# Seven-product pairs in two of three down projections, other start addresses for their operands, and their additions moved to the end of the group

## The chip, the cores and the metric

The kernel runs on one core of a Trainium2 chip. It computes two transformer-like blocks on 256 tokens of width 2048, in float32 precision. The metric is the device time of one execution in microseconds (us). Before the change the median of three runs is 2616.38 us (2616.24 to 2616.57).

## The reference, cut to what matters

The change touches only the second block's feed-forward part, at the very end of the program. The hidden width is 5632 and the model width 2048:

```
hn = rms_norm_2(h, norm_ffn_g)
gate, up = jnp.split(hn @ w_gate_up, 2, axis=-1)
h = h + (jax.nn.silu(gate) * up) @ w_down
out = rms_norm_2(h, norm_final_g)
```

## The kernel before, in words

**Precision.** Every float32 operand is split into a high part (what the matmul's float32r format keeps) and a low part (the rest). A product is three matmuls: high by high, high by low, low by high. Weights arrive by DMA in `raw` (4 slots of two pieces each, 1 MB a slot), ScalarE copies a piece to `hi` (line 577), VectorE subtracts to get `lo` (line 941). `hi` and `lo` are rings of 4 pieces. The splits run 3 pieces ahead of TensorE (`AHEAD`), and a piece's `hi` and `lo` may be written only when TensorE has used the piece four before it.

**A piece** is 256 rows of a weight matrix by 512 columns. A group is one block of 512 output columns over all rows of a stage. Groups alternate between PSUM banks 0 to 3 and 4 to 7.

**The end of the program** is six stages: `f2_up0`, `f2_down0`, `f2_up1`, `f2_down1`, `f2_up2`, `f2_down2`. An up stage computes four (the last: three) blocks of 512 hidden columns, and the down stage behind it multiplies these by their rows of `w_down` into four groups of 512 output columns. A group of `f2_down0` and `f2_down1` has 8 pieces, one of `f2_down2` has 6. In a down stage the tokens (in `B`, high and low part) are the stationary operand and the weights stream past, 512 columns at a time. An ordinary piece is 2 (blocks of 128 rows) by 2 (halves of the tokens) by 3 matmuls, lines 1616 to 1618. Three such matmuls, one of each line, are called a triple below; an ordinary pair of pieces is 8 triples.

**The seven-product pair.** Pieces 2 and 3 of every down group except the very last one are worked as a pair, by a Strassen-like scheme in `seven_products`: 2x2 blocks of tokens times 2x2 blocks of weights need 7 products in place of 8. That is 14 products of 3 matmuls, 42 matmuls of 256 columns (lines 1757 to 1759) in place of 24 of 512. Eleven pairs are worked so: 4 in `f2_down0`, 4 in `f2_down1`, 3 in `f2_down2`. They need:

- sums of the activations, `s_form`, once for each down stage. VectorE and ScalarE make them in `activation_sums`, behind the second `up` group of the up stage.
- sums of the weight blocks, `t_sum`, made in `block_sums` by four VectorE operations (lines 957 to 961) behind the split of piece 1, and split into `t_hi` (ScalarE, line 584) and `t_lo` (VectorE, line 945) behind the split of piece 3. The second of the four operations changes a raw block, so ScalarE's split of piece 2 waits for it.
- five VectorE additions (lines 969 to 974) and one ScalarE copy (line 589) in `combine`, which bring two extra PSUM banks into the result `HT`. They stand at piece 5 of the group (`j == SEVEN_AT + 3`). The result's other two banks are added at the group's end (`evacuate`, kind `tpart` or `tlast`, line 1174).

At the end of a `tlast` group (`f2_down2`) VectorE also waits for ScalarE's squares of the result (line 650) and multiplies by the final gain (line 1186), before it goes on splitting. The very last group is worked in two token halves (`last_pieces`, lines 1805 to 1807).

**Order.** Each engine's program is written out by `walk`: for piece p it first splits up to piece p+3, then does what belongs to p. So at the last piece of a group an engine splits piece 2 of the next group, then evacuates the group, then splits piece 3 of the next and the block sums.

**Addresses.** SBUF tensors lie one behind the other in the order of their declarations, each start rounded up to 32 bytes. From the declared sizes: `hi` and `lo` have the same start modulo 256; call it 0. Then `A` and the rows of `B` start at -64 (`B` is 67,776 bytes behind `hi`, 264 x 256 + 192, and a row of `B` is 9 x 256 bytes). The tokens start `TOKEN_AT` = 16 floats into a row, so at 0. `s_form` is at -64, and `t_hi` and `t_lo` are at +64 (167,232 bytes behind `hi`, 653 x 256 + 64).

Of the kernel before, what the change touches and what calls it, by code (L numbers as in the profile page):

```python
# [45 lines left out]
TOKEN_AT = 16  # L46
# [203 lines left out]
def bass_two_blocks(nc, ins, out):  # L250
    SEGS, TOTAL = schedule()
    PAIRS = seven_product_pairs(SEGS)

    with ExitStack() as ctx:
# [26 lines left out]
        s_form, t_sum = overlay(s_form=([P, 2, 4, 2, P], F32R), t_sum=[P, 2, 3, SEVEN_COLS])  # L281
# [8 lines left out]
        small = sb("small", [P, 64])  # L290
        r_fin = sb("r_fin", [P, T])
# [18 lines left out]
        _, t_hi, t_lo = overlay(gfin_end=[P, MT * T + 3 * D], t_hi=([P, 2, 3, SEVEN_COLS], F32R), t_lo=([P, 2, 3, SEVEN_COLS], F32R))  # L310
# [185 lines left out]
        def walk(eng, tallies, split, evacuate, side, each_turn, combine, activation_sums, last):  # L496

            at = {"split": AHEAD}  # L500

            for seg in SEGS:
                def run(turn, t):
                    base = seg.p0 + (t or 0) * seg.per_turn

                    def split_to(end):

                        while at["split"] < end:
                            n = turn * seg.per_turn + seg.p0 + at["split"]
                            if not isinstance(n, int) or n < TOTAL:  # L510
                                split(n, base + at["split"])
                            at["split"] += 1

                    for g, kind in enumerate(seg.kinds):
                        G = turn * len(seg.kinds) + seg.g0 + g
                        for j in range(seg.pieces):
                            p = g * seg.pieces + j
                            split_to(p + 1 + AHEAD)
                            b0 = 4 * ((seg.g0 + g + (t or 0) * len(seg.kinds)) % 2)
                            if t is not None and j == SEVEN_AT + 3 and base + g * seg.pieces + SEVEN_AT in PAIRS:  # L520
                                combine(PAIRS[base + g * seg.pieces + SEVEN_AT], b0, turn * len(seg.kinds) + g)
                            if j == seg.pieces - 1:
# [8 lines left out]
                                evacuate(kind, G, end, b0, turn * len(seg.kinds) + g, first_tile(seg, turn, g), more,  # L531
                                         token_parts if seg.name.startswith("f2") else B_parts)
                                if sums:
                                    activation_sums(more)
                                assert left[0] == 0, (kind, left)
                            if (seg.name, p) in EACH_TURN:
                                each_turn(EACH_TURN[seg.name, p], turn)
                            if t is not None and t == 0:
                                for step in SIDE.get((seg.name, p), ()):
                                    side(step, G, lambda: split_to(at["split"] + 1))  # L540
                    at["split"] -= seg.per_turn


                lead = 0
                if seg.turns > 1:
                    steady = AHEAD + MORE.get(seg.kinds[-1], 0)
                    lead = 0 if at["split"] == steady else 1
                turns_of(eng, seg, tallies, run, lead)
            last()


        @block.scalar
        def _(act):
# [12 lines left out]
            def split(n, slot):  # L566

                raw_slot = slot // 2 % RAWS
                if isinstance(n, int):
                    act.wait_ge(raw_landed[raw_slot], landed(n // 2))  # L570
                elif slot % 2 == 0 or slot < AHEAD:
                    act.wait_ge(raw_landed[raw_slot], turn_landed(n, slot))
                if not isinstance(n, int) or n >= RING:
                    act.wait_ge(pieces_used, n - RING + 1)
                if isinstance(n, int) and n in PAIRS:
                    act.wait_ge(t1_set, PAIRS[n] + 1)
                act.activation(hi[:, slot % RING], raw[:, raw_slot, 2 * (slot % 2):2 * (slot % 2) + 2, :],  # L577
                               ACT.Copy).then_inc(hi_ready, 1)
                if isinstance(n, int) and n - 1 in PAIRS:
                    q = PAIRS[n - 1]  # L580
# [10 lines left out]
            def activation_sums(more):  # L591
# [3 lines left out]
                given.mark(act.activation(s_form[:, 0], pb_copy[:, :, :].rearrange("p f (i c) -> p f i c", i=2), ACT.Copy))  # L595
# [25 lines left out]
            def evacuate(kind, G, end, b0, gi, k, more, to_b):  # L621
# [294 lines left out]
            walk(act, {1: asked, 2: given, 3: ready}, split, evacuate, side, lambda quarter, turn: None, combine, activation_sums, last)  # L916
# [3 lines left out]
        def _(dve):  # L920
# [15 lines left out]
            def split(n, slot):  # L936
# [6 lines left out]
                if isinstance(n, int) and n - 1 in PAIRS:  # L943
                    dve.wait_ge(t_hi_ready, PAIRS[n - 1] + 1)
# [4 lines left out]
            def block_sums(n):  # L949

                w = raw[:, n // 2 % RAWS, :, :].rearrange("p (i e) (s c) -> p i e s c", e=2, s=2)
                dve.wait_ge(raw_landed[n // 2 % RAWS], landed(n // 2))
                dve.wait_ge(h_turned, 16)
                if PAIRS[n]:
                    dve.wait_ge(t_lo_ready, PAIRS[n])
# [6 lines left out]
                dve.wait_ge(t1_set, PAIRS[n] + 1)  # L962

            def combine(q, b0, gi):
# [6 lines left out]
                dve.tensor_tensor(x[:, 0, :], x[:, 0, :], work[:, 0:2, :].rearrange("p s c -> p (s c)"), ALU.add)  # L971
# [4 lines left out]
            def activation_sums(more):  # L976
# [10 lines left out]
                dve.tensor_tensor(s_form[:, 1], pb_copy[:, :, :].rearrange("p f (i c) -> p f i c", i=2), s_form[:, 0],  # L987
# [32 lines left out]
            def evacuate(kind, G, end, b0, gi, k, more, to_b):  # L1020
# [149 lines left out]
                elif kind in ("tpart", "tlast"):  # L1170
# [3 lines left out]
                    dve.tensor_tensor(x, x, ps[:, b0:b0 + 2, :], ALU.add).then_inc(psum_free, 1)  # L1174
# [343 lines left out]
            walk(dve, {0: own, 1: asked, 2: given, 3: ready}, split, evacuate, side, turn_h, combine, activation_sums, last)  # L1518
# [3 lines left out]
        def _(pe):  # L1522
# [71 lines left out]
            def piece(seg, g, j, slot, b0, n, steps=None):  # L1594
# [7 lines left out]
                for kk in range(2):  # L1602
                    k = 2 * j + kk + (4 * WIDEST_FIRST[g] if seg.name == "pool" else 0)
                    first = j == 0 and kk == 0
                    final = (j == seg.pieces - 1 or isinstance(n, int) and n == TOTAL - RING - 1) and kk == 1
# [145 lines left out]
            def seven_products(j, slot, b0, n):  # L1751

                Xh, Xl = token_parts
                half = SEVEN_COLS

# [8 lines left out]
                def summed(f, i):  # L1764
                    return s_form[:, 0, f, i, :], s_form[:, 1, f, i, :]
# [9 lines left out]
                pe.wait_ge(s_ready, PAIRS[n] // 4 + 1)  # L1775
                for i in range(2):
                    k = 2 * (j + i)
                    pe.wait_ge(lo_ready, n + i + 1)
                    product(p16[:, 0:half], i == 0, False, tokens(0, k), *block(0, 0, i))
                    product(z0[:, 0:half], False, False, tokens(0, k + 1), *block(1, 0, i))  # L1780
                    product(z0[:, half:GC], False, False, summed(3, i), *block(1, 1, i))
                    product(p57[:, 0:half], i == 0, False, summed(0, i), *block(0, 1, i)).then_inc(pieces_used, 1)
                pe.wait_ge(t_lo_ready, PAIRS[n] + 1)
                for i in range(2):
                    k = 2 * (j + i)
                    product(p16[:, half:GC], False, i == 1, summed(1, i), *block_sum(1, i))
                    product(p57[:, half:GC], False, i == 1, summed(2, i), *block_sum(0, i))
                    last = product(z1[:, 0:half], False, False, tokens(1, k + 1), *block_sum(2, i))
# [24 lines left out]
            for seg in SEGS:  # L1813
                def run(turn, t):
                    for g, kind in enumerate(seg.kinds):
# [10 lines left out]
                        for j in range(seg.pieces - RING if at_end else seg.pieces):  # L1826
# [9 lines left out]
                            if isinstance(n, int) and n in PAIRS:  # L1836
                                seven_products(j, slot, b0, n)
# [47 lines left out]
```

## Time and profile before

| | us |
|---|---|
| median of 3 runs | 2616.38 |
| profiled execution | 2616.46 |
| its span | 2614.7 |
| `f2_down0`, TensorE | 2061.4 to 2146.5 |
| `f2_down1`, TensorE | 2321.1 to 2406.2 |
| `f2_down2`, TensorE | 2537.2 to 2607.6 |
| tail behind the last matmul | 2607.6 to 2614.7 |

The profiled execution takes 1.8 us more than its span (what lies before the first and behind the last recorded instruction). "Busy" is the time in which an engine had an instruction under way. A matmul is recorded with its latency, longer than its share of the stream; the rate is read from the starts of successive matmuls.

### The profile page before, as it was taken

To read this page: it belongs to the slowest core of one execution; us is meant where nothing else is said; L and a number is where in the kernel's file an instruction comes from. 1 tells how busy PE (TensorE), PEld (TensorE's weight loads), DVE (VectorE), ACT (ScalarE), POOL (GpSimd) and SP (SyncE) were. 2 spreads that over 40 slices of the span, in tenths; PEclk is the share of its full clock that TensorE was granted. 3 is DMA by queue.
4 is the path that set the end of the run, shared out by engine and by line. 5 is a ranking of instruction groups with operands and counts; after the bars stand their busy time and mean duration, and the time that the engine had idled before them with its cause. 6 is when DMAs were issued, how large, how long until landed. Compare 5 with 4: busy or idle time off the path is not lost.

```text
span 2614.7 us, 50642 instructions
## 1 busy us (share of the span) xinstructions
PE 2602.3 (100%) x21534; PEld 2551.2 (98%) x21534; DVE 1694.6 (65%) x1817; ACT 1187.4 (45%) x1284; POOL 14.6 (1%) x33
## 2 busy tenths in 40 slices
PE   9999999999999999999999999999999999999998
PEld 8989999999999999999999999999999989998997
DVE  7668765555555556795676666556777875677567
ACT  5356554434443444465443433444544444444444
POOL 2000000000000000000000000000000000000000
PEclk9999999999999999999999999999999999999999
DMA  9654566565655565555555555555565555556553
GB/s 306 202 168 163 196 193 196 187 201 187 200 186 200 188 199 193 179 203 195 180 184 189 193 182 190 193 193 194 193 210 194 193 198 193 191 195 205 194 179 129
DMA packets 254461, 504.31 MB, mean 193 GB/s; under 512 B 9390, under 2 KB 11456, under 8 KB 254160
## 3 DMA queue, kind: packets, MB, share of 16 engines
q1 hardware_dynamic: 250160, 496.27, 56.8%
q10 hardware_dynamic: 3136, 4.21, 0.5%
q8 instruction: 131, 2.15, 0.3%
q0 software_dynamic: 992, 1.34, 0.2%
q14 instruction: 42, 0.34, 0.0%
HBM read 498.89 MB, written 2.89 MB: 192 GB/s over the span
## 4 chain that ended last, share of the span: by engine, by line
PE 99%; DVE 1%; issue 0%; ACT 0%; POOL 0%; DVEq 0%; ACTq 0%; POOLq 0%
PE ps L1579 49%; PE ps L1590 25%; PE ps L1637 4%; PE ps L1646 4%; PE ps L1641 3%; PE ps L1616 3%; PE ps L1618 3%; PE ps L1617 3%; PE ps L1757 1%; PE ps L1759 1%; PE ps L1758 1%; PE ps L1626 1%; PE ps L1627 1%; PE ps L1624 1%; DVE lo L941 0%
## 5 line engine op out<-in xcount | busy, mean ns | idle before, releaser
L941 DVE TENSOR_TENSOR lo<-raw,hi 128x1024 fp32r<-128x1024 f32 x939 | 1139.7, 1224 | 792.6 <-ACT hi L577 779.2
L577 ACT ACTIVATE hi<-raw 128x1024 fp32r<-128x1024 f32 x939 | 988.4, 1059 | 1208.0 <-PE ps L1590 924.3
L1579 PE MATMUL ps<-A,hi 128*128 128x256 f32 x7286 | 902.8, 276 | 0.0
L1579 PEld LDWEIGHTS ps<-A,hi 128*128 128x128 f32 x7286 | 861.1, 188 | 0.3
L1579 PE MATMUL ps<-B,hi 128*128 128x256 f32 x3963 | 491.0, 276 | 0.0
L1590 PE MATMUL ps<-A,lo 128*128 128x256 f32 x3648 | 487.7, 276 | 0.0
L1579 PEld LDWEIGHTS ps<-B,hi 128*128 128x128 f32 x3963 | 468.3, 188 | 0.1
L1590 PEld LDWEIGHTS ps<-A,lo 128*128 128x128 f32 x3648 | 447.5, 188 | 0.0
L1590 PE MATMUL ps<-B,lo 128*128 128x256 f32 x1984 | 265.2, 276 | 0.0
L1590 PEld LDWEIGHTS ps<-B,lo 128*128 128x128 f32 x1984 | 243.3, 188 | 0.0
L1637 PE MATMUL ps<-B,hi 128*128 128x260 f32 (+3 forms) x768 | 109.1, 284 | 0.0
L1646 PE MATMUL ps<-B,lo 128*128 128x258 f32 (+3 forms) x768 | 108.7, 284 | 0.0
L1641 PE MATMUL ps<-B,hi 128*128 128x256 f32 x768 | 104.1, 278 | 0.0
L1637 PEld LDWEIGHTS ps<-B,hi 128*128 128x128 f32 x768 | 100.0, 189 | 0.0
L1646 PEld LDWEIGHTS ps<-B,lo 128*128 128x128 f32 x768 | 98.9, 189 | 0.0
L1616 PE MATMUL ps<-hi,B 128*128 128x512 f32 x248 | 96.8, 390 | 0.0
L1618 PE MATMUL ps<-hi,B 128*128 128x512 f32 x248 | 96.6, 389 | 0.0
L1617 PE MATMUL ps<-lo,B 128*128 128x512 f32 x248 | 96.5, 389 | 0.0
L1641 PEld LDWEIGHTS ps<-B,hi 128*128 128x128 f32 x768 | 96.3, 188 | 0.0
L676 ACT ACTIVATE B<-work 128x1024 f32 (+1 forms) x26 | 27.6, 1063 | 72.5 <-DVE work L1081 64.6
L1618 PEld LDWEIGHTS ps<-hi,B 128*128 128x128 f32 x248 | 46.5, 188 | 10.0
L1617 PEld LDWEIGHTS ps<-lo,B 128*128 128x128 f32 x248 | 46.6, 188 | 9.2
(306 smaller groups left out, 1589.5 us busy)
## 6 DMA issues: line engine op xcount, KB each, us to landing
raw<-in_w_in_dram SPq DMA_DIRECT2D x135, 1024.0 KB, 5.1
raw<-in_ffn_w_dram SPq DMA_DIRECT2D x132, 1024.0 KB, 5.1
raw<-in_w_gate_up_dram SPq DMA_DIRECT2D x88, 1024.0 KB, 5.0
raw<-in_w_down_dram SPq DMA_DIRECT2D x44, 1024.0 KB, 5.0
raw<-in_w_out_dram SPq DMA_DIRECT2D x16, 1024.0 KB, 5.1
raw<-in_pl_w_gate_dram SPq DMA_DIRECT2D x16, 1024.0 KB, 5.1
raw<-in_conv_out_w_dram SPq DMA_DIRECT2D x16, 1024.0 KB, 5.0
raw<-in_w_o_dram SPq DMA_DIRECT2D x16, 1024.0 KB, 5.0
```

The source lines that it names most:

```text
L577: act.activation(hi[:, slot % RING], raw[:, raw_slot, 2 * (slot % 2):2 * (slot % 2) + 2, :], ACT.Copy).then_inc(hi_ready, 1)
L676: given.mark(act.activation(some((A_parts if kind == "cb" else to_b)[0], k, 4, 0, T), work[:, :, :], ACT.Copy))
L941: dve.tensor_tensor(lo[:, slot % RING], raw[:, slot // 2 % RAWS, 2 * (slot % 2):2 * (slot % 2) + 2, :], hi[:, slot % RING], ALU.subtract). ...
L1579: pe.matmul(ps[:, b0 + m, 0:T], high(slot, kk, m), x, start=j == 0 and kk == 0 and part == 0, stop=False)
L1590: last = pe.matmul(ps[:, b0 + m, 0:T], low(slot, kk, m), Xh, start=False, stop=j == seg.pieces - 1 and kk == 1)
L1616: pe.matmul(to, Xh, hi[:, slot % RING, kk, :], start=first, stop=False)
L1617: pe.matmul(to, Xh, lo[:, slot % RING, kk, :], start=False, stop=False)
L1618: last = pe.matmul(to, Xl, hi[:, slot % RING, kk, :], start=False, stop=final)
L1624: pe.matmul(to, Wh, Xh, start=first and m % 2 == 0, stop=False, skip_group_check=True)
L1637: pe.matmul(ps[:, b0 + m, 0:with_lo], high(slot, kk, m), B[:, 2 * j + kk, 0:with_lo], start=first and kk == 0, stop=False, skip_group_chec ...
L1641: pe.matmul(ps[:, b0 + m, 0:T], high(slot, kk, m), B_low[:, 2 * j + kk, :], start=False, stop=False, skip_group_check=True)
L1646: last = pe.matmul(ps[:, b0 + m, 0:with_hi], low(slot, kk, m), B[:, 2 * j + kk, 0:with_hi], start=False, stop=final and kk == 1, skip_grou ...
```

## The change

Four things are changed.

1. The pairs are now listed by stage, `PAIRS_AT`, for `f2_down0` and `f2_down1` alone. The three pairs of `f2_down2` become ordinary pieces, and the activation sums behind `f2_up2` go.
2. Addresses: `TOKEN_AT` becomes 0, so the tokens start at -64 in the count above. `t_hi` and `t_lo` start 48 floats (192 bytes) later, at 0. `s_form` has room for a second set (not used) and keeps its start; `t_sum` moves to the place of `r_fin`, `sumsq` and the tensors behind them, and `block_sums` no longer waits until `h` has been transposed.
3. `combine` moves from piece 5 to the group's end. VectorE first adds the two ordinary banks (as line 1174 did), then makes the five additions; the last of them frees the banks.
4. The start and stop flags and the indices are written for a list of pairs (`u` counts them in a group); with one pair in a group they come out as before.

```diff
-TOKEN_AT = 16
+TOKEN_AT = 0
...
-SEVEN_AT = 2
+PAIRS_AT = {"f2_down0": (2,), "f2_down1": (2,)}
+SUMS_BEHIND = {"f2_up0": (1,), "f2_up1": (1,)}
...
+def down_groups(segs):
+    return [(x, x.p0 + turn * x.per_turn + g * x.pieces)
+            for x in segs if x.name in PAIRS_AT for turn in range(2) for g in range(2)]
...
-    first = [x.p0 + turn * x.per_turn + g * x.pieces + SEVEN_AT
-             for x in segs if x.name.startswith("f2_down") for turn in range(2) for g in range(2)]
-    return {n: q for q, n in enumerate(first[:-1])}
+    pairs, groups = {}, {}
+    for i, (x, first) in enumerate(down_groups(segs)):
+        for u, j in enumerate(PAIRS_AT[x.name]):
+            pairs[first + j] = (len(pairs), sum(len(PAIRS_AT[f"f2_down{c}"]) for c in range(int(x.name[-1]))) + u, u)
+        groups[first] = (i, len(pairs) - 1)
+    return pairs, groups
...
-        s_form, t_sum = overlay(s_form=([P, 2, 4, 2, P], F32R), t_sum=[P, 2, 3, SEVEN_COLS])
+        s_form, = overlay(s_form=([P, 2, 2, 4, 2, P], F32R))
...
+        t_sum, = overlay(t_sum=[P, 2, 3, SEVEN_COLS])
         r_fin = sb("r_fin", [P, T])
...
-        _, t_hi, t_lo = overlay(gfin_end=[P, MT * T + 3 * D], t_hi=...
+        _, t_hi, t_lo = overlay(gfin_end=[P, MT * T + 3 * D + 48], t_hi=...
...
-                            if t is not None and j == SEVEN_AT + 3 and base + g * seg.pieces + SEVEN_AT in PAIRS:
-                                combine(PAIRS[base + g * seg.pieces + SEVEN_AT], b0, turn * len(seg.kinds) + g)
                             if j == seg.pieces - 1:
-                                sums = seg.name.startswith("f2_up") and kind == "up" and t == SEVEN_AT // 2
+                                behind = SUMS_BEHIND.get(seg.name, ())
+                                sums = kind == "up" and t in behind
+                                seven = SEVEN_GROUPS.get(base + g * seg.pieces) if t is not None else None
...
             def block_sums(n):
...
-                dve.wait_ge(h_turned, 16)
...
-            def combine(q, b0, gi):
-                x = HT[:, :, gi * GC:(gi + 1) * GC]
+            def combine(c, q, b0, x):
                 p1, v5, v7, u2 = (work[:, i, :] for i in range(4))
-                dve.wait_ge(p1_copied, q + 1)
+                dve.wait_ge(t_used, q + 1)
+                own.mark(dve.tensor_tensor(x, x, ps[:, b0:b0 + 2, :], ALU.add))
+                dve.wait_ge(p1_copied, c + 1)
                 step(dve.tensor_tensor(u2, p1, ps[:, b0 + 2, SEVEN_COLS:GC], ALU.add))
...
-                step(dve.tensor_tensor(x[:, 1, SEVEN_COLS:GC], x[:, 1, SEVEN_COLS:GC], ps[:, b0 + 3, 0:SEVEN_COLS], ALU.add))
+                return dve.tensor_tensor(x[:, 1, SEVEN_COLS:GC], x[:, 1, SEVEN_COLS:GC], ps[:, b0 + 3, 0:SEVEN_COLS], ALU.add)
...
-                    dve.tensor_tensor(x, x, ps[:, b0:b0 + 2, :], ALU.add).then_inc(psum_free, 1)
+                    if seven:
+                        combine(*seven, b0, x).then_inc(psum_free, 1)
+                    else:
+                        dve.tensor_tensor(x, x, ps[:, b0:b0 + 2, :], ALU.add).then_inc(psum_free, 1)
```

## Rows read from the trace of the kernel before

**Rows 1.** The page, parts 1 (busy time of each engine) and 4 (last chain).

```profile
PE 2602.3 (100%) x21534; PEld 2551.2 (98%) x21534; DVE 1694.6 (65%) x1817; ACT 1187.4 (45%) x1284; POOL 14.6 (1%) x33
...
PE 99%; DVE 1%; issue 0%; ACT 0%; POOL 0%; DVEq 0%; ACTq 0%; POOLq 0%
```

**Rows 2.** Windows, `f2_down2`: us, PE, PEld, DVE, ACT, POOL busy, PEclk, DMA share, GB/s.

```profile
2537.00:2607.70 70.70, 66.96 (x345) 56.93 (x344) 58.68 (x69) 34.04 (x48) 0.00 (x0) 0.98 0.34 122
```

**Rows 3.** Timeline, TensorE, pairs 2 and 3 of `f2_down2`: start, duration, instruction, idle before.

```profile
2558.47 0.28 PE L1757 MATMUL ps<-hi,B 128*128 128x256 f32 x1
...
2562.01 0.39 PE L1757 MATMUL ps<-hi,B 128*128 128x256 f32 x1 [1.99 <-DVE lo L941]
...
2567.31 0.40 PE L1616 MATMUL ps<-hi,B 128*128 128x512 f32 x1
...
2578.23 0.28 PE L1757 MATMUL ps<-hi,B 128*128 128x256 f32 x1
...
2580.60 0.39 PE L1757 MATMUL ps<-hi,B 128*128 128x256 f32 x1 [0.82 <-DVE lo L941]
...
2584.56 0.40 PE L1616 MATMUL ps<-hi,B 128*128 128x512 f32 x1
```

**Rows 4.** Windows: a part of pair 2 of `f2_down2`.

```profile
2563.36:2566.77 3.41, 3.41 (x17) 3.25 (x17) 3.41 (x4) 2.32 (x3) 0.00 (x0) 0.50 0.82 295
```

**Rows 5.** Timeline, TensorE, the last group of `f2_down2`.

```profile
2596.61 0.39 PE L1807 MATMUL ps<-hi,B 128*128 128x512 f32 x1
2597.80 0.50 PE L1805 MATMUL ps<-hi,B 128*128 128x512 f32 x1 [0.80 <-DVE lo L941]
```

**Rows 6.** Timeline, VectorE, end of the first group of `f2_down2`.

```profile
2556.97 1.22 DVE L1174 TENSOR_TENSOR HT<-HT,ps 128x1024 f32<-128x1024 f32 x1
2559.60 1.23 DVE L1186 TENSOR_TENSOR HT<-HT,gfin_row 128x1024 f32<-128x1024 f32 x1 [1.40 <-ACT pb_copy L650]
```

**Rows 7.** Timeline, TensorE, the pair of the second group of `f2_down0`.

```profile
2088.13 0.28 PE L1757 MATMUL ps<-hi,B 128*128 128x256 f32 x1
...
2088.84 0.28 PE L1757 MATMUL ps<-hi,s_form 128*128 128x256 f32 x1
...
2089.52 0.28 PE L1757 MATMUL ps<-hi,B 128*128 128x256 f32 x1
...
2090.92 0.28 PE L1757 MATMUL ps<-t_hi,s_form 128*128 128x256 f32 x1
...
2093.05 0.40 PE L1616 MATMUL ps<-hi,B 128*128 128x512 f32 x1
```

**Rows 8.** Timeline, TensorE, `f2_down0`: two starts with 36 matmuls between them.

```profile
2117.77 0.39 PE L1616 MATMUL ps<-hi,B 128*128 128x512 f32 x1
...
2125.93 0.39 PE L1616 MATMUL ps<-hi,B 128*128 128x512 f32 x1
```

**Rows 9.** Timeline, TensorE, stage `g`: two starts with 42 matmuls between them.

```profile
151.15 0.39 PE L1616 MATMUL ps<-hi,A 128*128 128x512 f32 x1
...
160.77 0.39 PE L1616 MATMUL ps<-hi,A 128*128 128x512 f32 x1
```

**Rows 10.** Timeline, ScalarE, first group of `f2_down0`: high part of the next group's piece 1.

```profile
2077.51 1.06 ACT L577 ACTIVATE hi<-raw 128x1024 fp32r<-128x1024 f32 x1 [1.39 <-PE ps L1618]
```

**Rows 11.** Timeline, VectorE, from piece 5 of the first group of `f2_down0`.

```profile
2077.02 0.41 DVE L969 TENSOR_TENSOR work<-work,ps 128x256 f32<-128x256 f32 x1
...
2079.98 1.23 DVE L941 TENSOR_TENSOR lo<-raw,hi 128x1024 fp32r<-128x1024 f32 x1
...
2083.80 1.23 DVE L941 TENSOR_TENSOR lo<-raw,hi 128x1024 fp32r<-128x1024 f32 x1
2084.94 1.21 DVE L1174 TENSOR_TENSOR HT<-HT,ps 128x1024 f32<-128x1024 f32 x1
2086.07 1.22 DVE L941 TENSOR_TENSOR lo<-raw,hi 128x1024 fp32r<-128x1024 f32 x1
2087.21 1.75 DVE L945 TENSOR_TENSOR t_lo<-t_sum,t_hi 128x1536 fp32r<-128x1536 f32 x1
```

More of the change, by code:

```diff
@@ L494, in first_tile, with walk @@
             return (turn * len(seg.kinds) + g) * MT
-        def walk(eng, tallies, split, evacuate, side, each_turn, combine, activation_sums, last):
+        def walk(eng, tallies, split, evacuate, side, each_turn, activation_sums, last):
             at = {"split": AHEAD}
@@ L531, in run @@
                                 evacuate(kind, G, end, b0, turn * len(seg.kinds) + g, first_tile(seg, turn, g), more,
-                                         token_parts if seg.name.startswith("f2") else B_parts)
+                                         token_parts if seg.name.startswith("f2") else B_parts, seven)
                                 if sums:
-                                    activation_sums(more)
+                                    activation_sums(more, behind.index(t))
                                 assert left[0] == 0, (kind, left)
@@ L594, in activation_sums @@
                 wait(asked)
-                given.mark(act.activation(s_form[:, 0], pb_copy[:, :, :].rearrange("p f (i c) -> p f i c", i=2), ACT.Copy))
+                given.mark(act.activation(s_form[:, u, 0], pb_copy[:, :, :].rearrange("p f (i c) -> p f i c", i=2), ACT.Copy))
             def turn_landed(n, slot):
@@ L619, in residual_out, with evacuate @@
                 ready.skip()
-            def evacuate(kind, G, end, b0, gi, k, more, to_b):
+            def evacuate(kind, G, end, b0, gi, k, more, to_b, seven):
+                if seven:
+                    combine(*seven, b0)
                 if kind == "cg":
@@ L914, in last @@
                         act.dma_start(out[0, a * P:(a + 1) * P, c:e], HT[:, a, c:e]).then_inc(stored, 16)
-            walk(act, {1: asked, 2: given, 3: ready}, split, evacuate, side, lambda quarter, turn: None, combine, activation_sums, last)
+            walk(act, {1: asked, 2: given, 3: ready}, split, evacuate, side, lambda quarter, turn: None, activation_sums, last)
         @block.vector
@@ L1018, in residual_out, with evacuate @@
                 ready.mark(dve.tensor_tensor(some(A, k, 4, T, 2 * T), hk, some(A, k, 4, 0, T), ALU.subtract))
-            def evacuate(kind, G, end, b0, gi, k, more, to_b):
+            def evacuate(kind, G, end, b0, gi, k, more, to_b, seven):
                 Rm = row_of(R, MT)
@@ L1516, in last @@
                         dve.tensor_scalar(HT[:, a, c:e], HT[:, a, c:e], r, None, ALU.mult).then_inc(left_scaled, 1)
-            walk(dve, {0: own, 1: asked, 2: given, 3: ready}, split, evacuate, side, turn_h, combine, activation_sums, last)
+            walk(dve, {0: own, 1: asked, 2: given, 3: ready}, split, evacuate, side, turn_h, activation_sums, last)
         @block.tensor
@@ L1749, in side, with seven_products @@
                         done.mark(last)
-            def seven_products(j, slot, b0, n):
+            def seven_products(seg, j, slot, b0, n):
                 Xh, Xl = token_parts
                 half = SEVEN_COLS
+                q, sums, u = PAIRS[n]
+                closes = j == seg.pieces - 2
+                last_pair = u == 1 or n + 4 not in PAIRS
                 def product(to, start, stop, x, w_hi, w_lo):
@@ L1778, in seven_products @@
                     pe.wait_ge(lo_ready, n + i + 1)
[L1779 to L1783, printed above, removed]
+                    product(p16[:, 0:half], u == 0 and i == 0, False, tokens(0, k), *block(0, 0, i))
+                    product(z0[:, 0:half], False, closes and i == 1, tokens(0, k + 1), *block(1, 0, i))
+                    product(z0[:, half:GC], False, closes and i == 1, summed(3, i), *block(1, 1, i))
+                    product(p57[:, 0:half], u == 0 and i == 0, False, summed(0, i), *block(0, 1, i)).then_inc(pieces_used, 1)
+                pe.wait_ge(t_lo_ready, q + 1)
                 for i in range(2):
                     k = 2 * (j + i)
-                    product(p16[:, half:GC], False, i == 1, summed(1, i), *block_sum(1, i))
-                    product(p57[:, half:GC], False, i == 1, summed(2, i), *block_sum(0, i))
-                    last = product(z1[:, 0:half], False, False, tokens(1, k + 1), *block_sum(2, i))
+                    product(p16[:, half:GC], False, last_pair and i == 1, summed(1, i), *block_sum(1, i))
+                    product(p57[:, half:GC], False, last_pair and i == 1, summed(2, i), *block_sum(0, i))
+                    last = product(z1[:, 0:half], False, closes and i == 1, tokens(1, k + 1), *block_sum(2, i))
                 last.then_inc(t_used, 1)
```

36 lines of the change are left out of this document (19 added, 17 removed).

## The prediction, made before the changed kernel was run

> **What bounds the kernel now.** The page first: TensorE has work under way in 2602.3 of 2614.7 us, and the chain that ended last is TensorE for 99% [rows 1]. So a change is worth what it does to TensorE's stream: the number of matmuls, the time from one start to the next, and the gaps. Then the windows of the three down stages, which are all that the change touches: in `f2_down2` TensorE is busy 66.96 of 70.70 us and its clock has a mean of 0.98 [rows 2], so there is a place with stops. In `f2_down0` and `f2_down1` its timeline has no idle entry. Last, starts of single matmuls, since the recorded durations are latencies. They give five prices.
>
> - An ordinary pair of pieces in a down stage: 36 matmuls of 512 columns take 2125.93 - 2117.77 = 8.16 us [rows 8], 0.2267 each, 0.680 a triple, 24 of them 5.44 us.
> - A seven-product pair that doesn't wait: 2093.05 - 2088.13 = 4.92 us [rows 7]. It is worth 0.52 us.
> - Pair 2 of `f2_down2`: 2567.31 - 2558.47 = 8.84 us; pair 3: 2584.56 - 2578.23 = 6.33 us [rows 3]. Both wait for VectorE's `lo`, 1.99 and 0.82 us of idle time. Behind the longer wait the granted clock is 0.50, that is 1.2 in place of 2.4 GHz, for 3.41 us [rows 4]; this is why 1.99 us of waiting cost 3.92. Pair 1 runs like rows 7, at 4.92.
> - In the last group TensorE waits for `lo` once more: start to start 2597.80 - 2596.61 = 1.19, less 0.23 of matmul, 0.96 us [rows 5], and the next start is 0.11 late: 1.07 us.
>
> Why these waits: VectorE is full around a group's end. The add of line 1174 waits for ScalarE's squares to be done with it, and then comes the gain; from its start to the gain's end 2559.60 + 1.23 - 2556.97 = 3.86 us [rows 6]. Ahead of these 3.86 us stand the five additions and, with a group of only 6 pieces, the block sums and `t_lo` of the next pair.
>
> **Part 1: no pairs in `f2_down2`.** Removed: 4.92 + 8.84 + 6.33 = 20.09 us. Added: 3 x 5.44 = 16.32. Gain 3.77. The work that made VectorE late (per pair five additions 2.96 us, four block sums 2.68, `t_lo` 1.67, by starts [rows 11]) goes too. What is late next? At a group's end TensorE has three pieces ready, 3 x 2.72 = 8.2 us. VectorE needs some 0.2 for the release, 3.86 [rows 6] and one split of 1.23, together 5.3, so it comes 2.9 us early. In the last group TensorE runs two pieces and half of a third (6.8 us) before it needs the `lo` that is ready at 5.3. So the 1.07 us goes. Between ends: it could stay whole (0), I take it as gone. A pair leaves the first triples behind it a little slow, worth 0.04 us each; 0.1 more. The activation sums behind `f2_up2` are hidden there already, TensorE has no idle entry beside them: 0. Part 1: -3.77 - 1.07 - 0.1 = **-4.9 us**.
>
> **Part 2: addresses.** Within one pair the rows show two rates. The six matmuls with moving `hi` and stationary tokens (both at 0) take 2088.84 - 2088.13 = 0.71; the six with stationary `s_form` (at -64) take 2089.52 - 2088.84 = 0.68. The 18 with moving `t_hi` and `t_lo` (at +64) take 2093.05 - 2090.92 = 2.13, or 0.118 each against 0.1133 [rows 7]. After the change `hi` and `t_hi` are at 0, and tokens and `s_form` at -64: every one of the 42 has the relation of the fast six. 42 x 0.1134 = 4.76, or 0.16 less than 4.92. For 8 pairs -1.3 us (lower end: 0, if only chance separates them; I take the whole, for the rates repeat within the pair).
>
> But the ordinary pieces get their tokens from -64 too. The same three lines with a stationary operand at -64 and `hi` at 0 are seen in stage `g`, where it is `A`: 42 matmuls take 160.77 - 151.15 = 9.62 us, 0.2290 each, 0.687 a triple against 0.680 [rows 9, 8]. After the change 8 groups have 24 ordinary triples and 4 groups have 24: 288. 288 x 0.687 less 288 x 0.680 is 2.0; in the groups with pairs, the slow triples behind a pair (0.04 each time, 0.3 in all) would no longer stand out: +1.7 us. The ends are 0 and +2.0. I take **+1.7**, the nearest row: same lines, same shapes, same offset; only the row length differs (2048 bytes against 2304), and both are multiples of 256. Part 2 together is **+0.4 us**: the ordinary pieces give back what the pairs gain.
>
> The Trainium skill says otherwise on both: in "SBUF — State Buffer", section "Who interferes with whom", TensorE has two independent read ports for the moving operand and the weight load, and only the pair of ports that VectorE shares with GpSimd makes anyone wait. By that rule the address of an operand cannot matter and part 2 is 0. The trace doesn't agree as far as 0.71 against 0.68 us within one pair goes.
>
> **Part 3: additions at the group's end.** In `f2_down0` and `f2_down1` VectorE's work is the same in sum, but its order changes: the 2.96 us leave piece 5 and stand behind the add of line 1174, before the split of the next group's piece 3 and `t_lo`, which the next pair needs. So I write out one boundary, that of groups 1 and 2 of `f2_down0`. `hi` of the next piece 1 is ready at 2077.51 + 1.06 = 2078.57 [rows 10]; in the kernel before `lo` started only at 2079.98, behind the additions [rows 11]. Now it starts at 2078.61. Split and block sums take 2083.80 - 2079.98 = 3.82, so `lo` of piece 2 starts at 2082.43; its `hi` waits for the second block sum, and is ready at about 2082.3. The add of line 1174 starts 1.14 later, at 2083.57 (TensorE is through with the group by 2082.9), the five additions 1.13 later, at 2084.70, `lo` of piece 3 at 2087.66, `t_lo` at 2088.80, with its end at 2090.55 all steps by [rows 11]. TensorE wants `lo` of piece 3 at 2088.13 + 0.71 + 0.68 = 2089.5 (ready 2088.9), and `t_lo` at 2088.13 + 24 x 0.1134 = 2090.85 [rows 7]. It is ready 0.3 us before. Queued behind: the split of piece 4 ends 1.2 us later, at 2091.7, and is wanted at 2092.9. So the six boundaries with a pair behind them cost 0, with little cover: each 0.1 us by which the chain is longer than 0.3 costs 0.6 us. Bounds: 0 to 6 x 0.4 = 2.4 us. The two boundaries towards an up stage have no pair behind them; there 5.3 us of VectorE work meet 8.2 us of ready pieces. The banks come free 3 us later, but are next wanted a whole group later. ScalarE's copy of line 589 is read long after it is made. The wait for `h_turned` that goes was met long before. SyncE refills a `raw` slot when the `lo` of both pieces is made; that is up to 1.6 us later at a boundary, with a transfer of 5 us wanted some 13 us later: 0.
>
> **Sum.** -4.9 + 0.4 + 0 = -4.5 us. Profiled execution 2616.46 to 2612.0; the median of before lies 0.08 lower, so **2611.9 us**. A measurement tells about 0.2% (5.2 us) from no change, so anything under 2611.15 counts as faster: the forecast is real but just inside "the same".
>
> **Rivals.**
>
> - *Ordinary pieces stay at 0.680.* Then part 2 is -1.3 and the sum -6.2: 2610.2, faster. For it: the 512-column matmuls of before, with tokens and `hi` at the same residue, showed nothing of what the 256-column ones did, so shape matters and the length of the row might. Against: rows 9 are very regular. Chance 0.17.
> - *Addresses don't matter at all*: the stream and the weight load never meet, part 2 is 0, the sum -4.9, 2611.5. The differences in rows 7 and 9 would then come from what is multiplied. Chance 0.12. (It is the rule of the Trainium skill, "SBUF — State Buffer", named in part 2.)
> - *A short wait at each boundary.* The chain of part 3 is longer by 0.35 to 0.7 us: 0.3 to 2.4 us lost, 2612.2 to 2614.3. For it: 0.3 us of cover in twelve steps. Chance 0.13.
> - *The moved additions become the bound, slower than before.* It is the mechanism of rows 3: VectorE late at a group's end, TensorE waits for `lo` or `t_lo`, and the clock may fall. If each of six boundaries costs what pair 3 cost, 6.33 - 4.92 = 1.41 us, the loss is 8.5 and the sum +4.0: 2620.4. It decides from 4.5 / 6 = 0.75 us of waiting per boundary, that is from a chain 1.05 us longer than written out; one more VectorE operation of 1.2 us in it would do. Against it: every duration has a row and none is missing. Chance 0.03.
> - *The change doesn't do what it says*: for one pair in a group the flags come out as before; nothing speaks for it.
>
> **How the numbers follow.** The forecast has 0.55. Faster by over 0.2%: the first rival whole (0.17), a third of the second (0.04), and 0.05 of the forecast's own spread: 0.26. Slower: 0.03 and 0.01 for what I don't see. The same: 0.70. The range goes from the first rival's time less 0.2 to where the short waits are mostly in: 2610.0 to 2613.6.
>
> **What the changed kernel's profile would show.** In `f2_down2` no line 1757, no idle entry on TensorE and a clock of 1.00; the stage some 66 us from first to last matmul in place of 70.4. A pair of `f2_down0` 4.76 us long, its six-matmul steps all 0.68. Triples of lines 1616 to 1618 at 0.687. On VectorE the additions behind the whole add, `t_lo` ending some 0.3 us before the first matmul that streams it. The forecast is wrong if triples stay at 0.680, if the pairs stay at 4.92, or if TensorE shows idle entries before `t_hi` in `f2_down0` and `f2_down1`.

## The result, and the profile after

The changed kernel takes 2625.33 us (median of 7 runs, 2625.28 to 2625.64) against 2616.43 before: ratio 1.0034, 95% interval 1.0022 to 1.0046. It is 8.9 us slower, and the forecast was 2611.9, range 2610.0 to 2613.6. Lines of the changed kernel stand 13 to 22 further down: 1598 and 1609 are the up stages' matmuls (before 1579 and 1590), 1635 to 1637 the ordinary triples (1616 to 1618), 1779 to 1781 the pairs (1757 to 1759), 590 ScalarE's split (577), 956 VectorE's split (941), 960 `t_lo` (945), 983 the add of the two ordinary banks (1174, now in `combine`).

The page first: busy times and the last chain of the changed kernel, beside [rows 1].

```profile
PE 2614.1 (100%) x21480; PEld 2558.7 (98%) x21480; DVE 1672.0 (64%) x1782; ACT 1184.1 (45%) x1277; POOL 14.6 (1%) x33
...
PE 99%; DMA 0%; DVE 0%; ACT 0%; issue 0%; SPq 0%; DVEq 0%; ACTq 0%
```

TensorE has 54 matmuls fewer and is busy 11.8 us longer. Nothing else on the page moved by more than the removed work. So the question is where the stream runs slower. Windows of the last five stages of the changed kernel, in order `f2_down0`, `f2_up1`, `f2_down1`, `f2_up2`, `f2_down2` (columns as in [rows 2]):

```profile
2061.36:2146.32 84.96, 84.96 (x458) 73.14 (x457) 67.81 (x70) 41.17 (x41) 0.00 (x0) 1.00 0.57 199
2146.32:2327.66 181.34, 181.34 (x1541) 181.33 (x1540) 101.76 (x92) 75.81 (x72) 0.00 (x0) 1.00 0.56 187
2327.66:2412.93 85.27, 85.27 (x458) 73.35 (x457) 67.60 (x70) 41.17 (x41) 0.00 (x0) 1.00 0.57 198
2412.93:2548.93 136.00, 136.00 (x1156) 136.00 (x1155) 73.17 (x63) 55.99 (x53) 0.00 (x0) 1.00 0.57 186
2548.93:2616.29 67.36, 67.36 (x290) 54.25 (x288) 40.04 (x42) 30.16 (x41) 0.00 (x0) 1.00 0.36 126
```

and the same five of the kernel before:

```profile
2061.39:2146.53 85.14, 85.14 (x459) 73.77 (x457) 70.56 (x75) 40.48 (x41) 0.00 (x0) 1.00 0.56 193
2146.53:2321.10 174.57, 174.57 (x1542) 174.57 (x1540) 98.82 (x87) 75.69 (x72) 0.00 (x0) 1.00 0.59 196
2321.10:2406.23 85.13, 85.13 (x458) 73.76 (x457) 70.56 (x75) 40.49 (x41) 0.00 (x0) 1.00 0.56 193
2406.23:2537.17 130.94, 130.94 (x1156) 130.93 (x1155) 74.58 (x67) 56.91 (x54) 0.00 (x0) 1.00 0.59 196
2537.17:2607.64 70.47, 66.79 (x344) 56.76 (x342) 58.51 (x69) 34.01 (x47) 0.00 (x0) 0.98 0.34 121
```

The down stages moved by -0.18, +0.14 and -3.11 us. By the prediction's terms they should have moved by about -0.1, -0.1 and -4.2 (-4.9 of part 1 and 96 triples x 0.007), so the first is as forecast and the last lost 1.1 us of its gain. And the two up stages, whose matmuls the change doesn't touch, take 181.34 - 174.57 = 6.77 and 136.00 - 130.94 = 5.06 us more, 11.83 together. Same number of matmuls, TensorE busy throughout, granted clock 1.00 in both: each matmul starts 0.1178 us behind the last in place of 0.1134. The sum, -0.18 + 6.77 + 0.14 + 5.06 - 3.11 = 8.7, is the difference of the spans (8.8).

The steps inside the down stages, TensorE's timeline of the changed kernel: a pair of `f2_down0`, first triples and first pair of `f2_down1`, and two triples of `f2_down2`.

```profile
2071.62 0.39 PE L1635 MATMUL ps<-hi,B 128*128 128x512 f32 x1
...
2088.10 0.28 PE L1779 MATMUL ps<-hi,B 128*128 128x256 f32 x1
...
2092.86 0.39 PE L1635 MATMUL ps<-hi,B 128*128 128x512 f32 x1
...
2327.66 0.40 PE L1635 MATMUL ps<-hi,B 128*128 128x512 f32 x1
...
2333.26 0.28 PE L1779 MATMUL ps<-hi,B 128*128 128x256 f32 x1
...
2338.21 0.40 PE L1635 MATMUL ps<-hi,B 128*128 128x512 f32 x1
...
2548.93 0.40 PE L1635 MATMUL ps<-hi,B 128*128 128x512 f32 x1
...
2593.74 0.40 PE L1635 MATMUL ps<-hi,B 128*128 128x512 f32 x1
```

In `f2_down0` 24 triples take 2088.10 - 2071.62 = 16.48 us, 0.687 each, as forecast from [rows 9]; the pair takes 2092.86 - 2088.10 = 4.76. But in `f2_down1` the first eight triples take 5.60, 0.700 each, and the first pair 4.95; behind that pair it is like `f2_down0`. In `f2_down2`, 64 triples take 2593.74 - 2548.93 = 44.81, 0.700 each, and it stays so to the end. So the same instruction on the same tensors goes at two paces, and the slower one is seen behind the two slow up stages.

VectorE's chain at the boundary written out in the prediction, in the changed kernel, and the first matmul that needs it:

```profile
2078.46 1.23 DVE L956 TENSOR_TENSOR lo<-raw,hi 128x1024 fp32r<-128x1024 f32 x1 [1.52 <-ACT hi L590]
...
2083.43 1.22 DVE L983 TENSOR_TENSOR HT<-HT,ps 128x1024 f32<-128x1024 f32 x1
...
2088.53 1.75 DVE L960 TENSOR_TENSOR t_lo<-t_sum,t_hi 128x1536 fp32r<-128x1536 f32 x1
```

```profile
2090.82 0.28 PE L1779 MATMUL ps<-t_hi,s_form 128*128 128x256 f32 x1
```

`t_lo` ends at 2090.28, 0.54 us before it is wanted (forecast 0.3), and TensorE has no idle entry anywhere in these stages.

### The profile page after: what moved, and what is told of

It reads as the page before. It is cut to its first block, busy times and chain, and to the rows that moved or that the text cites. A ratio compares the mean times of both kernels' runs of the same rounds, so it can differ in the third digit from the quotient of the medians.

```text
span 2623.5 us, 50481 instructions
## 1 busy us (share of the span) xinstructions
PE 2614.1 (100%) x21480; PEld 2558.7 (98%) x21480; DVE 1672.0 (64%) x1782; ACT 1184.1 (45%) x1277; POOL 14.6 (1%) x33
## 4 chain that ended last, share of the span: by engine, by line
PE 99%; DMA 0%; DVE 0%; ACT 0%; issue 0%; SPq 0%; DVEq 0%; ACTq 0%
PE ps L1598 49%; PE ps L1609 25%; PE ps L1656 4%; PE ps L1665 4%; PE ps L1637 4%; PE ps L1635 4%; PE ps L1636 4%; PE ps L1660 3%; PE ps L1645 1%; PE ps L1646 1%; PE ps L1643 1%; PE ps L1781 0%; PE ps L1779 0%; PE ps L1780 0%; DMA raw<-in_w_in_dram 0%; PE ps L1829 0%
## 5 line engine op out<-in xcount | busy, mean ns | idle before, releaser
L1637 PE MATMUL ps<-hi,B 128*128 128x512 f32 x272 | 107.5, 395 | 0.0
L1636 PE MATMUL ps<-lo,B 128*128 128x512 f32 x272 | 107.1, 394 | 0.0
L1635 PE MATMUL ps<-hi,B 128*128 128x512 f32 x272 | 106.4, 391 | 0.0
L1635 PEld LDWEIGHTS ps<-hi,B 128*128 128x128 f32 x272 | 51.2, 188 | 11.1
L1637 PEld LDWEIGHTS ps<-hi,B 128*128 128x128 f32 x272 | 51.2, 188 | 10.8
```

What stands on the lines that cost most here:

```text
L1635: pe.matmul(to, Xh, hi[:, slot % RING, kk, :], start=first, stop=False)
L1636: pe.matmul(to, Xh, lo[:, slot % RING, kk, :], start=False, stop=False)
L1637: last = pe.matmul(to, Xl, hi[:, slot % RING, kk, :], start=False, stop=final)
```

## The experiments

The theory after the result: **inherited pace**. It says that a stream of like matmuls has more than one pace; the pace is settled in the first matmuls behind a change of shape, and then kept. What the down stage's stream leaves, together with one odd matmul at the start of each pair of groups of `f2_up1` and `f2_up2`, settles it. That odd matmul is in both kernels: `EVERY_TURN` cuts the first low-part product at column 248 into one of 248 and one of 8 columns. The prediction does not mention it.

split_half, no_split, before_no_split, sums_place, late_cut and first_cut_only were executed once each, and no_split later 11 times more. The executions of one kernel lie within 1.1 us of each other, and the two paces of the up stages are 11.8 us apart.

**tokens_back.** The tokens' address alone undone.

```diff
-TOKEN_AT = 0
+TOKEN_AT = 16
```

> The changed kernel (2625.3 us) with one line undone: the tokens start 16 floats into a row of B again, at the residue of hi; everything else stays changed. In the changed kernel's trace the 2695 matmuls of f2_up1 and f2_up2 start 0.118 us apart in place of 0.113, worth some 11.9 us, and all triples of f2_down2 take 0.700. Theory 'inherited pace': a stream of like matmuls has several paces, and which one it keeps is settled by the stream ahead of it; the tokens' address changed the stream of the down stages, and with it the pace that the up stages behind them fall into. It expects the up stages at 0.113, ordinary triples at 0.680, pairs between 4.76 and 4.92 us, and 2616.4 - 4.9 - 0.6 = 2610.9 us. Rival 'the sums' place': the new places of t_sum, t_hi and t_lo, or the additions at the group's end, make the up stages slow; then they stay at 0.118 and the time is about 2623.

Measured: 2611.12 us, ratio 0.9981 (0.9971 to 0.9990). `f2_up1` takes 174.57 us again, triples 0.680, pairs 4.87.

```profile
2146.26:2320.83 174.57, 174.57 (x1542) 174.57 (x1540) 101.43 (x92) 75.71 (x72) 0.00 (x0) 1.00 0.58 193
```

The sums' new place and the moved additions are still there and the up stages are fast. So these two do not make them slow; the tokens' new start does, with the cuts as they are.

**before_tokens.** The same line changed in the kernel before.

```diff
-TOKEN_AT = 16
+TOKEN_AT = 0
```

> The kernel before with one line changed: the tokens start at the beginning of a row of B (64 bytes before the residue of hi). Pairs, sums and the place of the additions are as before. Theory 'inherited pace', with the tokens' address as what changes the down stages' stream: ordinary triples at 0.687, f2_up1 and f2_up2 at 0.118 or another pace than 0.113, so 2616.4 + 1.6 + 11.9, less 0.6 for the pairs, some 2629 us. Rival 'the sums' place': the up stages stay at 0.113, and the time is 2616 to 2618.

Measured: 2628.74 us, ratio 1.0047 (1.0031 to 1.0064). The two up stages:

```profile
2147.01:2328.35 181.34, 181.34 (x1542) 181.34 (x1540) 99.13 (x87) 75.81 (x72) 0.00 (x0) 1.00 0.57 189
2414.16:2550.16 136.00, 136.00 (x1156) 136.00 (x1155) 74.97 (x67) 56.82 (x54) 0.00 (x0) 1.00 0.57 190
```

To the hundredth the durations of the changed kernel. One number in one line makes 12.5 us. The pairs of `f2_down0` did not gain what was expected: they take 4.85 and 4.96 us in turn, against 4.92 before.

**split_half and no_split.** The changed kernel with another cut, and with none.

```diff
-EVERY_TURN = {("f2_up1", 0): (0, 248), ("f2_up2", 0): (0, 248), ("conv", 16): ...
+EVERY_TURN = {("f2_up1", 0): (0, P), ("f2_up2", 0): (0, P), ("conv", 16): ...      (split_half)
+EVERY_TURN = {("conv", 16): (0, P), ("conv", 40): (0, P)}                          (no_split)
```

> The changed kernel, but the one matmul that is cut in two at the start of every group pair of f2_up1 and f2_up2 is cut at column 128 and not at column 248. The number of columns and all addresses are the same. Theory 'inherited pace': the cut shifts the stream against the weight loads, so another cut can put it in another pace; it expects f2_up1 and f2_up2 to change pace as a whole, to 0.113 if the cut hits (then some 2613.5 us), or to some third value. Rival 'direct contention': the up stages' reads meet writes of VectorE and ScalarE to the new token addresses; then a cut changes nothing and both stages stay at 0.118, 2625.3 us.

> The changed kernel without the cut matmuls of f2_up1 and f2_up2: the first matmul of each pair of groups goes out whole. Theory 'inherited pace': the first matmuls of f2_up1 keep whatever pace the down stage leaves them in, a pace of 0.1135 to 0.120, the same through the whole stage; if it is 0.113 the time falls to some 2613. Rival 'direct contention': unchanged at 0.118 but for the 7 cuts, some 0.6 us less, 2624.7.

Measured: 2615.64 and 2611.05 us. no_split's two up stages:

```profile
2146.32:2320.43 174.11, 174.11 (x1538) 174.11 (x1536) 101.45 (x92) 75.69 (x72) 0.00 (x0) 1.00 0.58 194
2405.39:2535.97 130.58, 130.58 (x1153) 130.58 (x1152) 73.09 (x63) 55.96 (x53) 0.00 (x0) 1.00 0.58 194
```

The tokens still lie at -64, VectorE and ScalarE write them as before, and the stages are fast: direct contention with these writes is out. In split_half both expectations missed: the pace changes in the middle of a stage. The first pair of groups of `f2_up1` is slow, the next one fast:

```profile
2146.66:2192.40 45.74, 45.74 (x390) 45.73 (x389) 24.81 (x24) 18.17 (x18) 0.00 (x0) 1.00 0.57 190
2193.20:2236.00 42.80, 42.80 (x380) 42.80 (x379) 23.37 (x21) 18.06 (x19) 0.00 (x0) 1.00 0.57 187
```

45.74 us for 389 weight loads is 0.118 each, 42.80 for 379 is 0.113. The cut at 128 that opens the second pair of groups (2192.5) lies between them, and `f2_up2` changes at its second cut too. In the changed kernel the cut at 248 in the same place changes nothing. So a cut can lift a slow stream into the fast pace; the first cut at 128, right behind the down stage, did not.

**before_no_split.** The kernel before without the cuts.

```diff
-EVERY_TURN = {("f2_up1", 0): (0, 248), ("f2_up2", 0): (0, 248), ("conv", 16): ...
+EVERY_TURN = {("conv", 16): (0, P), ("conv", 40): (0, P)}
```

> The kernel before without the cut matmuls of f2_up1 and f2_up2. Theory 'inherited pace': with tokens at the residue of hi the stream enters the up stages in another phase than in the changed kernel, in which the cut is what brings it to 0.113; without the cuts f2_up1 and f2_up2 go at a slower pace, 0.118 or near, 2616.4 + 11.9 = 2628 us. Rival: a cut is harmful or idle everywhere; then 2616.4 less 7 x 0.1 = 2615.7 us.

Measured: 2627.25 us. Its `f2_up1` and `f2_up2`:

```profile
2146.55:2327.46 180.91, 180.91 (x1537) 180.90 (x1536) 99.15 (x87) 75.77 (x72) 0.00 (x0) 1.00 0.57 188
2412.58:2548.26 135.68, 135.68 (x1153) 135.68 (x1152) 74.91 (x67) 56.81 (x54) 0.00 (x0) 1.00 0.57 190
```

In the kernel before, the cuts are worth 10.9 us. With tokens at 0 the cut makes the stage fast and its absence slow; with tokens at -64 it is the other way round:

| | cut at 248 | no cut |
|---|---|---|
| tokens at 0 | before 2616.4, fast | before_no_split 2627.3, slow |
| tokens at -64 | changed 2625.3, slow | no_split 2611.1, fast |

(The upper row has the pairs of `f2_down2`, the lower one not; that is worth 4.6 us, see two_downs.)

The entry into `f2_up1` shows it. TensorE's timeline of the kernel before, from the first up matmul:

```profile
2146.53 0.63 PE L1579 MATMUL ps<-A,hi 128*128 128x256 f32 x4
2147.00 0.28 PE L1577 MATMUL ps<-A,hi 128*128 128x248 f32 x2
2147.14 1.51 PE L1579 MATMUL ps<-A,hi 128*128 128x256 f32 x11
2148.49 0.73 PE L1590 MATMUL ps<-A,lo 128*128 128x256 f32 x5
```

of the changed kernel:

```profile
2146.32 0.64 PE L1598 MATMUL ps<-A,hi 128*128 128x256 f32 x4
2146.80 0.28 PE L1596 MATMUL ps<-A,hi 128*128 128x248 f32 x2
2146.94 1.54 PE L1598 MATMUL ps<-A,hi 128*128 128x256 f32 x11
2148.32 0.87 PE L1609 MATMUL ps<-A,lo 128*128 128x256 f32 x6
```

and of no_split and before_no_split, each with the 16 matmuls merged in one row:

```profile
2146.32 2.00 PE L1598 MATMUL ps<-A,hi 128*128 128x256 f32 x16
2148.16 1.07 PE L1609 MATMUL ps<-A,lo 128*128 128x256 f32 x8
```

```profile
2146.55 2.05 PE L1579 MATMUL ps<-A,hi 128*128 128x256 f32 x16
2148.44 0.75 PE L1590 MATMUL ps<-A,lo 128*128 128x256 f32 x5
```

16 matmuls to the next line's first: 1.84 us without a cut and tokens at -64, 1.89 with tokens at 0. Before the cut both kernels are slow (2147.00 - 2146.53 = 0.47 for four, about 0.118 each; 0.48 in the changed one). Behind it the kernel before needs 2148.49 - 2147.14 = 1.35 us for eleven, the changed one 1.38.

The single starts in these traces show where the ways part. In no_split the interval from the fourth to the fifth matmul of the stage is 0.123 us, and from the sixth matmul on the intervals are 0.113 to 0.114. In the changed kernel the same 0.123 stands in the same place, but the cut comes right behind it. Once past the two cut matmuls, all intervals are 0.115 to 0.119. In the kernel before the first four intervals are 0.117 to 0.118; past the cut comes one of 0.122, and then the fast pace. In before_no_split no long interval comes, and the stage stays slow. In split_half an interval of 0.123 stands behind the second cut, ahead of the fast pace. So each of these streams that became fast did so behind one interval of 0.122 to 0.123 us. With tokens at 0 the cut brings that interval in, and with tokens at -64 a cut right behind it undoes it. Why, no run shows.

The down stage behind a slow up stage takes up the slow pace only with tokens at -64. In before_no_split the first eight triples of `f2_down1` take 2332.90 - 2327.46 = 5.44 us, 0.680 each, as behind a fast stage.

**two_downs and sums_place.** Two more parts alone, in the kernel before.

```diff
-             for x in segs if x.name.startswith("f2_down") for turn in range(2) for g in range(2)]
-    return {n: q for q, n in enumerate(first[:-1])}
+             for x in segs if x.name in ("f2_down0", "f2_down1") for turn in range(2) for g in range(2)]
+    return {n: q for q, n in enumerate(first)}
...
-                                sums = seg.name.startswith("f2_up") and kind == ...
+                                sums = seg.name in ("f2_up0", "f2_up1") and kind == ...      (two_downs)
...
-        _, t_hi, t_lo = overlay(gfin_end=[P, MT * T + 3 * D], ...
+        _, t_hi, t_lo = overlay(gfin_end=[P, MT * T + 3 * D + 48], ...                       (sums_place)
```

> The kernel before with one part of the change: no pairs and no activation sums for f2_down2. Addresses and the place of the additions are as before. The prediction's part 1 by itself: -3.8 (three pairs), -1.1 (the wait in the last group), -0.1, so 2616.4 - 4.9 = 2611.5 us, no idle entry and a clock of 1.00 in f2_down2. Rival: TensorE is held there by something else behind VectorE's pair work (ScalarE's squares, the gain), then a wait of up to 1 us stays and the time is 2612.5 or more. For the pace of the up stages both expect 0.113, since neither the tokens nor the cut is touched.

> The kernel before with t_hi and t_lo 48 floats later, at the residue of hi, and nothing else. Theory 'inherited pace' with the tokens' address as the cause of the slow up stages: the pairs go from 4.92 to 4.87 us as in tokens_back, the up stages stay at 0.113, 2616.4 - 11 x 0.05 = 2615.8 us, or up to 1 us off, as the waits of f2_down2 may move. Rival: this step alone turns the up stages to 0.118, 2628 us.

Measured: two_downs 2611.79 us, ratio 0.9983 (0.9973 to 0.9993). Its `f2_down2`:

```profile
2537.13:2602.59 65.46, 65.46 (x290) 53.87 (x288) 40.03 (x42) 30.14 (x41) 0.00 (x0) 1.00 0.37 130
```

No idle entry, clock 1.00, 65.46 us for 70.47: part 1 is worth 4.6 to 5.0 us, as forecast. sums_place: 2616.00 us, up stages at 174.57 and 130.94. The pairs of its `f2_down0` take 4.87, as expected. Neither run touches the pace of the up stages.

**late_cut and first_cut_only.** Where does the cut do its harm? The changed kernel with a single cut in the ninth piece of `f2_up1`, and with cuts only in the very first matmuls of `f2_up1` and `f2_up2`.

```diff
-EVERY_TURN = {("f2_up1", 0): (0, 248), ("f2_up2", 0): (0, 248), ("conv", 16): ...
+EVERY_TURN = {("conv", 16): (0, P), ("conv", 40): (0, P)}
...
-              ("f2_up0", 8): (0, P), ("ga", 8): (0, P)}
+              ("f2_up0", 8): (0, P), ("ga", 8): (0, P), ("f2_up1", 8): (0, 248)}                         (late_cut)
+              ("f2_up0", 8): (0, P), ("ga", 8): (0, P), ("f2_up1", 0): (0, 248), ("f2_up2", 0): (0, 248)}  (first_cut_only)
```

> The changed kernel without the cuts of f2_up1 and f2_up2 (2611.05 us as no_split), but with a single cut, at column 248, in the first matmul of the ninth piece of f2_up1. Theory 'inherited pace', sharpened: the cut itself throws the stream from 0.113 into 0.118, and it stays there until a matmul of another shape comes. It expects the first 192 matmuls of f2_up1 at 0.113 and the 1344 behind the cut at 0.118 (+5.9 us), f2_down1's first triples at 0.700 and its first pair at 4.95 (+0.3), f2_up2 at 0.113: 2617.3 us. Rival: a cut does harm only where the stream has just come from the 512-column matmuls; then this one costs its 0.1 us and the time is 2611.2. Second rival: the pace falls back by itself within a group; then between.

> The changed kernel with the cut at column 248 only in the very first matmul of f2_up1 and of f2_up2; the other five cuts are gone. After the late cut did no harm inside a fast stream, the theory says: the pace is settled in the first matmuls behind the down stage, where the cut meets the entry of the changed kernel at the wrong moment, and is then kept without any further cut. It expects both stages at 0.118 throughout, 2625.3 less 5 x 0.1 = 2624.8 us. Rival: each later cut renews the slow pace, and without them the stream falls back to 0.113 in some group; then between 2611.5 and 2622.

Measured: late_cut 2611.50, `f2_up1` 174.22 us: only the cut's own 0.11 (the rest of the 0.45 to no_split lies ahead of the stage). My sharpened theory, that the cut throws any fast stream into the slow pace, fell; its rival was right. first_cut_only 2624.81, as expected:

```profile
2146.38:2327.39 181.01, 181.01 (x1538) 181.01 (x1537) 101.65 (x92) 75.78 (x72) 0.00 (x0) 1.00 0.57 187
2412.66:2548.45 135.79, 135.79 (x1154) 135.78 (x1153) 73.08 (x63) 55.97 (x53) 0.00 (x0) 1.00 0.56 187
```

The first cut alone makes both stages slow, and they stay slow for 1536 and 1152 matmuls without another. The only difference to no_split is one cut at the head of each stage.

**additions_back.** The third part undone alone, in no_split: both engines' `combine` at piece 5 again, the plain add at the group's end.

```diff
+                            early = SEVEN_GROUPS.get(base + g * seg.pieces) if t is not None and j == 5 else None
+                            if early:
+                                combine(*early, b0, turn * len(seg.kinds) + g)
...
-                dve.wait_ge(t_used, q + 1)
-                own.mark(dve.tensor_tensor(x, x, ps[:, b0:b0 + 2, :], ALU.add))
+                x = HT[:, :, gi * GC:(gi + 1) * GC]
```

> no_split (the changed kernel without the cuts, 2611.1 us) with the additions back at piece 5 of the group, so the third part of the change is undone alone. In the changed kernel's trace t_lo of the second pair ends 0.54 us before the first matmul that streams it, and TensorE has no idle entry. The prediction's part 3 is then 0: 2611.1 us, same paces. Rival: the order on VectorE shifts the stream's pace as the tokens did; then some stage is at 0.118 and the time is 2615 us or more.

Measured: 2611.10 us, ratio 0.9980 (0.9971 to 0.9990). Against the 2611.09 of no_split_timed, part 3 costs nothing.

**no_split_timed and tokens_back_first_cut.** The two best, timed together. The first is no_split again; the second is:

```diff
-TOKEN_AT = 0
+TOKEN_AT = 16
-EVERY_TURN = {("f2_up1", 0): (0, 248), ("f2_up2", 0): (0, 248), ("conv", 16): ...
+EVERY_TURN = {("conv", 16): (0, P), ("conv", 40): (0, P)}
-              ("f2_up0", 8): (0, P), ("ga", 8): (0, P)}
+              ("f2_up0", 8): (0, P), ("ga", 8): (0, P), ("f2_up1", 0): (0, 248), ("f2_up2", 0): (0, 248)}
```

> The kernel of no_split, timed in rounds: tokens at -64 and no cut in f2_up1 and f2_up2. 2611.05 us as in the single look, ratio 0.9980. It is the changed kernel's nearest repair; ordinary triples at 0.687 and pairs at 4.76 us cost it 1.0 us against tokens at 0, and the cuts that it does without give back 0.8, so the first-cut version beats it by about 0.5.

> tokens_back (2611.1 us) with only the first cut of f2_up1 and of f2_up2. The same theory: the first cut brings the stream to 0.113 and it stays there, the five later cuts only cost their 0.115 each, so 2611.1 - 0.6 = 2610.5 us, ratio to the kernel before 0.9978. Rival, that every turn needs its cut: one of the stages falls to 0.118 from the second turn on, 2615 us or more.

Measured: 2611.09 us (ratio 0.9981, 0.9972 to 0.9990) and 2610.58 us (0.9979, 0.9970 to 0.9988). The second beats the kernel before by 5.7 us and the changed one by 14.8, and it shows that the later cuts of a stage are not needed.

## Why the prediction was wrong, step by step

- **What the change touches** is the step that failed. The prediction said that the windows of the three down stages "are all that the change touches", and priced each stage by itself. The runs showed 11.83 us in `f2_up1` and `f2_up2` behind them. The warning was in the trace before: the first four matmuls of `f2_up1` go at about 0.118, the rest of the stage at 0.1134. (The 0.113 and 0.118 of [rows 7] are no such warning by themselves, since the operands start elsewhere.) A price per matmul was taken for a property of the instruction and its addresses; it is also one of the stream's past. The same step put `f2_down2` too low: its 96 triples went at 0.700, not 0.687.
- **Part 1** (-4.9): right, by its own run. two_downs gives 2616.39 - 2611.79 = 4.6, the stage by itself 5.0.
- **Part 2, pairs** (4.76 us) **and ordinary triples** (0.687): right in `f2_down0`. In the changed kernel `f2_down2` runs at 0.700 behind the slow `f2_up2`, 96 triples x 0.013 = 1.2 us, and the start of `f2_down1` loses 0.3. Behind a fast up stage, in no_split, the triples are at 0.687 throughout. So the row from stage `g`, with other tensors, gave one of two possible paces; that it was the one of `f2_down0` was partly luck. The reasoning by single offsets holds less well than its result: the sums' move alone took a pair from 4.92 to 4.87 (sums_place), the tokens' move alone left it at 4.85 and 4.96 (before_tokens), both together gave 4.76.
- **Part 3** (0): right, shown by additions_back; the cover was 0.54 us.
- The rival "addresses don't matter at all" fell: before_tokens moves one address and is 12.5 us slower. By the Trainium skill, "SBUF — State Buffer", section "Who interferes with whom", TensorE's two read ports are independent and TensorE never waits on anyone. Taken as a rule for start addresses it would give 0, and the measured 12.5 us decide against that use of it; whether the ports have a part in them is not shown.
- The slower rival had the right side and the wrong mechanism: TensorE has no idle entry in these stages of the changed kernel.

Added up after the fact, the forecast and the terms that it lacked (the up stages, `f2_down2`, the start of `f2_down1`) give -4.5 + 11.8 + 1.2 + 0.3 = +8.8 us, measured +8.9.

## What to carry to other kernels

When a change shifts addresses or shapes in one stage of a TensorE-bound kernel, compare the start-to-start time of the matmuls in every later stage too, with the granted clock beside it: 4% on a stage that nobody edited cost over twice the planned gain. Where a kernel has an odd-looking cut or dummy instruction at the head of a stage, suspect that it sets the pace, and try it anew (with, without, elsewhere) after every change ahead of it.

## What the runs showed of the hardware that was not expected

- At a granted clock of 1.00 and with no waits, 256-column float32r matmuls keep one of two paces, 0.1134 or 0.1178 us, for over 1500 matmuls; triples of 512 columns showed 0.680 with tokens at 0, and 0.687 or 0.700 with tokens at -64.
- A single cut matmul (248 + 8 columns) at the head of a stage settled it: to the fast pace in tokens_back_first_cut, to the slow one in first_cut_only. It did nothing in the middle of a fast stream (late_cut). The five later cuts at 248 did not lift the changed kernel's slow streams; the second one at 128 did, in both up stages (split_half).
- What stays open: the mechanism. That the stream of moving columns and the weight loads fall into step with each other is a guess that no run tests. All that is shown is that the tokens' start and the cut together decide it, and that VectorE's order, the sums' place and the pairs of `f2_down2` did not where they were tried. Only two starts of the tokens, 64 bytes apart, were tried, so nothing shows that the start modulo 256 is what counts. Whether the last matmuls of the down stage are enough, or the whole stage counts, wasn't tried either.
